# Cached keys turned in 32x32 blocks by VectorE, and sample scores computed as 4x4 tiles

## The reference, cut to what matters

```
s_past = (ql . cp^T + qp . kp^T) * ATTN_SCALE     # 32 x 4096, contraction over 256 + 64
s_new  = (ql . cn^T + qp . kn^T) * ATTN_SCALE     # 32 x 4, causal
p = softmax(concatenate([s_past, s_new]))
out = p_past . cp + p_new . cn                    # 32 x 256
```

## Time and profile before

| | |
|---|---|
| runs, median of 3 (lowest to highest) | 1405.34 us (1402.3 to 1409.27) |
| profiled execution | 1393.17 us |
| its span, first to last instruction | 1391.2 us |
| granted TensorE clock, mean | 0.990 of full speed |
| TensorE busy | 1354.7 us, 97% |
| VectorE, ScalarE, GpSimd busy | 810.8, 601.3, 725.7 us |

### The profile page before, as it was taken

How to read it: one execution, slowest core, us unless ns; L and a number is a source line. 1 busy time by engine, 2 the same in 40 slices (tenths; PEclk the granted TensorE clock), 3 DMA queues, 4 the chain that set the end, 5 groups by cost and what they waited for, 6 DMA issues and landing times.

```text
span 1391.2 us, 26303 instructions
## 1 busy us (share of the span) xinstructions
PE 1354.7 (97%) x11048; PEld 1261.1 (91%) x11048; DVE 810.8 (58%) x1232; ACT 601.3 (43%) x1021; POOL 725.7 (52%) x505
## 2 busy tenths in 40 slices
PE   7999889999999999999999999999999999999997
PEld 7877489999999999999899867678999999999997
DVE  6689557655545463766556656554685463645434
ACT  5121255443434443444666544342464444443432
POOL 3321153587878785333323444330437788887831
PEclk9999789999999999999999999999999999999999
DMA  5755302222233324332111477770223322222221
GB/s 215 209 149 147 109 31 92 92 92 91 92 100 100 104 92 147 128 92 66 35 35 53 182 296 261 269 260 7 92 75 101 98 92 92 92 91 92 91 91 65
DMA packets 108356, 160.66 MB, mean 115 GB/s; under 512 B 7696, under 2 KB 93968, under 8 KB 102992
## 3 DMA queue, kind: packets, MB, share of 16 engines
q1 hardware_dynamic: 100688, 116.50, 26.4%
q0 software_dynamic: 7168, 41.95, 8.0%
q10 hardware_dynamic: 384, 0.55, 0.1%
HBM read 146.22 MB, written 4.03 MB: 108 GB/s over the span
## 4 chain that ended last, share of the span: by engine, by line
PE 91%; DVE 4%; ACT 1%; issue 1%; DMA 1%; POOL 1%; ACTq 0%; POOLq 0%; SPq 0%; DVEq 0%
PE ps L1675 31%; PE ps L1805 21%; PE ps L1793 18%; PE ps L1935 5%; PE ps L1975 3%; PE ps L1713 2%; PE ps L2024 2%; PE ps L1726 1%; PE ps L2091 1%; ACT wh L717 1%; PE ps L2005 1%; POOL wl L589 1%; PE ps L2015 1%; PE ps L2033 0%; PE ps L1763 0%
## 5 line engine op out<-in xcount | busy, mean ns | idle before, releaser
L589 POOL TENSOR_TENSOR wl<-raw,wh 128x512 fp32r<-128x512 f32 (+2 forms) x252 | 438.0, 1740 | 441.8 <-ACT wh L717 441.6
L717 ACT ACTIVATE wh<-raw 128x512 fp32r<-128x512 f32 (+2 forms) x253 | 192.6, 762 | 386.3 <-PE ps L1675 184.5
L1675 PE MATMUL ps<-xh,wh 128*128 128x272 f32 x704 | 148.4, 292 | 12.6 <-DVE xl L1084 10.0
L589 POOL TENSOR_TENSOR wl<-wuv,wh 128x512 fp32r<-128x512 f32 x104 | 135.0, 1310 | 48.2 <-ACT wh L717 48.1
L1805 PE MATMUL ps<-mh,wh 128*128 128x272 f32 x768 | 158.7, 288 | 0.0
L1805 PE MATMUL ps<-mh,wl 128*128 128x272 f32 x768 | 158.6, 288 | 0.0
L1805 PE MATMUL ps<-ml,wh 128*128 128x272 f32 x768 | 158.3, 288 | 0.0
L1675 PE MATMUL ps<-xh,wl 128*128 128x272 f32 x704 | 145.6, 289 | 0.0
L1675 PE MATMUL ps<-xl,wh 128*128 128x272 f32 x704 | 145.4, 288 | 0.0
L1675 PEld LDWEIGHTS ps<-xh,wh 128*128 128x128 f32 x704 | 110.6, 190 | 17.7 <-POOL wl L589 9.9
L1805 PEld LDWEIGHTS ps<-ml,wh 128*128 128x128 f32 x768 | 120.4, 188 | 0.0
(11 more groups left out here) (315 smaller groups left out, 3029.3 us busy)
## 6 DMA issues: line engine op xcount, KB each, us to landing
raw<-w_up SPq DMA_DIRECT2D x32, 1024.0 KB, 5.4
raw<-w_down SPq DMA_DIRECT2D x32, 1024.0 KB, 5.1
raw<-w_pw SPq DMA_DIRECT2D x11, 1024.0 KB, 5.8
shifted<-ext SPq DMA_DIRECT2D x112, 66.5 KB, 2.0
raw<-w_o SPq DMA_DIRECT2D x4, 1024.0 KB, 5.7
raw<-w_dq SPq DMA_DIRECT2D x3, 1024.0 KB, 5.4
raw<-w_uq SPq DMA_DIRECT2D x4, 768.0 KB, 4.7
diag<-diags SPq DMA_DIRECT2D x7, 384.0 KB, 3.5
```

Source lines behind the costliest of these rows:

```text
L589: pf.tensor_tensor(weight(wl, u), weight_raw(u), f32(weight(wh, u)), ALU.subtract).then_inc(w_lo, 1)
L717: af.activation(weight(wh, u), weight_raw(u), ACT.Copy).then_inc(w_hi, 1)
L1675: m = tf.matmul(ps[:, bank_of(u) + bank, 0:width], w[:, k, :], a[:, k, part], start=(k == 0 and n == 0), stop=(k == nk - 1 and n == 2))
```

## The change

VectorE's 32x32 block transpose takes the place of TensorE's transposes. `turn_keys(n)` turns a chunk from SBUF to SBUF in two instructions (2048 and 512 elements in each partition) into one of three slots (`KT`); afterwards the 32 features of block l lie on the 32 partitions of a row group, for the positions that came from that group. The score of a set is then ten blocks of 32 features in four row groups: 32x32 tiles, each row group into its own PSUM bank (4 to 7), each set on its own 32 columns. The queries must stand on all four row groups: `queries_turned` makes them by 40 matmuls with the identity ahead of the rounds, and ScalarE copies them to `qrep`. TensorE's loop becomes scores, fold, probability transposes and values of the same round. The scores have one set of banks, so those of round i + 1 wait for the exp of round i. ScalarE takes over `collect`, `folds` and `values_out` from VectorE. There are six chunk buffers for seven, and the gathers from chunk 3 on stand behind the last head's outputs and ahead of two `low(u)`.

```diff
-CB = 7
-ORDER = (0, 2, 1, 3, 4, 5, 7, 6, 8, 9)
+CB = 6
+KT = 3
+QB = (KL + ROPE) // 32
+FOLDS = SETS * SPB + 1
...
+        SCORES = ps[:, 4:8, 0:P]
+        FOLDED = ps[:, 0, 0:KC * NS]
+        PROBS, VALUES = ps[:, 1, :], ps[:, 3, :]
...  GpSimd
             gather(2)
-            gather(3)
...
+            pool.wait_ge(pv_mm, NH)
+            for j in range(3, CB):
+                gather(j)
             low(U_WO)
             low(U_WO + 1)
-            pool.wait_ge(pv_mm, NH)
-            for j in range(4, NCH):
-                gather(j)
+            for i in range(NSC):
+                for j in (CB + 2 * i, CB + 2 * i + 1):
+                    if j < NCH:
+                        gather(j)
...  ScalarE
+            def queries_out(m):
+                act.wait_ge(q_mm, m + 1)
+                af.activation(qrep[:, 2 * m:2 * m + 2, :, :].rearrange("p l b q -> p (l b q)"), ps[:, QBANK[m], :], ACT.Copy).then_inc(q_out, 1)
...
+            def folds(b):
+                act.wait_ge(e_wn, b + 1)
+                if b > 1:
+                    act.wait_ge(e_mm, b - 1)
+                for s in range(SETS):
+                    for k in range(SPB):
+                        af.activation(fold_w[NS * s:NS * (s + 1), b % 2, k, :], ident32, ACT.Copy, scale=wn[:, s, k:k + 1]).then_inc(e_fold, 1)
...
             for i in range(NSC):
+                if i > 0:
+                    values_out(i - 1)
+                if i > 0 and i % SPB == 0:
+                    weights_out(i // SPB - 1)
                 act.wait_ge(ks_max, i + 1)
-                af.activation(ss[:, :], ps[:, 3 + i % 2, :], ACT.Exp, ...
+                af.activation(ss[:, :].rearrange("p (q g k) -> p g q k", q=SETS, g=GROUPS), SCORES.rearrange("p g (q k) -> p g q k", q=SETS), ACT.Exp, ...
...
-                keys(i + 1, (0, 2, 4, 6, 8))
                 probs_out(i)
-                if i % SPB == SPB - 1:
-                    weights_out(i // SPB)
+                if i % SPB == SPB - 1:
+                    collect(i // SPB)
+                elif i > 0:
+                    folds(i // SPB - 1)
+            weights_out(NB - 1)
+            folds(NB - 1)
+            values_out(NSC - 1)
...  VectorE
+            def turn_keys(n, parts=(0, 1)):
+                if n >= NCH:
+                    return
+                for k in parts:
+                    if k == 0:
+                        dve.wait_ge(c_in[n % CB], 32 * (n // CB + 1))
+                        if n >= KT:
+                            dve.wait_ge(ks_mm, (n - KT) // 2 + 1)
+                    df.transpose(keys_turned(n)[k], (latents(n), rotaries(n))[k]).then_inc(kt_out, 1)
...
             for i in range(NSC):
+                turn_keys(2 * i + 2)
+                if i > 0 and i % SPB == 0:
+                    weights_first(i // SPB - 1)
                 dve.wait_ge(ks_mm, i + 1)
-                link(df.tensor_reduce(m, ps[:, 3 + i % 2, :], AX.X, ALU.max))
+                link(df.tensor_reduce(m, SCORES, AX.XY, ALU.max))
                 df.tensor_scalar(nmx[:, i % SETS:i % SETS + 1], m, -SCALE, None, ALU.mult).then_inc(ks_max, 1)
-                keys(i + 1, (1, 3, 5, 7, 9))
+                if i > 0 and i % SPB == 0:
+                    weights_second(i // SPB - 1)
+                turn_keys(2 * i + 3)
...  TensorE
+            def queries_turned(m):
+                if m == QB // 2 - 1:
+                    pe.wait_ge(q_out, 1)
+                for e in range(2):
+                    l = 2 * m + e
+                    for g in range(GROUPS):
+                        o = tf.matmul(ps[32 * g:32 * g + 32, QBANK[m], e * NB * NS:(e + 1) * NB * NS], ident[:, 32 * (l % 4):32 * (l % 4) + 32],
+                                      qs[:, l // 4, :, :].rearrange("p b q -> p (b q)"), start=True, stop=True)
+                o.then_inc(q_mm, 1)
...
-            def scores_s(i, c):
+            def scores_s(i):
                 b = i // SPB
-                pe.wait_ge(kt_act, 5 * i + (4, 5, 5)[c])
-                pe.wait_ge(kt_dve, 5 * i + (3, 4, 5)[c])
-                for s in range(SETS):
-                    q = qs[:, c if c < KC else KC + s % 2, b, :]
-                    k = kt[:, 5 * (s // 2) + (2 * (s % 2) + c if c < KC else 4), :]
-                    m = tf.matmul(ps[NS * s:NS * (s + 1), 3 + i % 2, :], q, k, start=(c == 0), stop=(c == 2))
+                pe.wait_ge(kt_out, 4 * i + 4)
+                if i == 0:
+                    pe.wait_ge(q_out, QB // 2)
+                    pe.wait_ge(n_max, 2)
+                else:
+                    pe.wait_ge(ks_exp, i)
+                for l in range(QB):
+                    for s in range(SETS):
+                        for g in range(GROUPS):
+                            rows_ = slice(32 * g, 32 * g + 32)
+                            m = tf.matmul(ps[NS * s:NS * (s + 1), 4 + g, 0:P], qrep[rows_, l, b, :], keys_block(2 * i + s // 2, s % 2, l)[rows_],
+                                          start=(l == 0), stop=(l == QB - 1))
+                m.then_inc(ks_mm, 1)
...
             for i in range(NSC):
-                for c in range(3):
-                    scores_s(i, c)
-                if i > 0:
-                    values(i - 1)
+                scores_s(i)
...
                 if i > SPB and i % SPB == 1:
                     folded(i // SPB - 1)
-                keys(i + 1, range(9))
+                if i == NSC - 1:
+                    out_first(U_WO, range(3))
                 probs_turned(i)
-                keys(i + 1, (9,))
+                if i == NSC - 1:
+                    out_first(U_WO, range(3, 5))
+                values(i)
```

More of the change, by code:

```diff
@@ L909, in rotary_samples @@
             def rotary_samples(n):
-                if n == 0:
-                    act.wait_ge(zeros, 2)
                 act.wait_ge(rq_out, n + 1)
                 for e in range(2):
[L914 to L918, removed]
+                    af.activation(qs[0:64, KC, :, NT * (2 * n + e):NT * (2 * n + e + 1)],
+                                  t0[64 * e:64 * e + 64, NP:T].rearrange("p (b t) -> p b t", t=NT), ACT.Copy).then_inc(kcopy, 1)
             def project(h):
@@ L991, in _ @@
                 else:
-                    keys(0, (0, 2))
+                    for m in range(QB // 2):
+                        queries_out(m)
                 pv_()
@@ L1007, in probs_out, with values_out, collect @@
                 act.wait_ge(kp_mm, i + 1)
-                af.activation(pts[:, :, :].rearrange("p a b -> p (a b)"), ps[:, 5, :], ACT.Copy).then_inc(kp_out, 1)
+                af.activation(pts[:, :, :].rearrange("p a b -> p (a b)"), PROBS, ACT.Copy).then_inc(kp_out, 1)
+            def values_out(i):
+                act.wait_ge(ko_mm, i + 2)
+                if i >= SETS:
+                    act.wait_ge(e_mm, (i - SETS) // SPB + 1)
+                af.activation(oc[:, i % SETS, :], VALUES[:, 0:KL], ACT.Copy).then_inc(ko_out, 1)
+            def collect(b):
+                act.wait_ge(ks_exp, SPB * (b + 1))
+                act.wait_ge(n_exp, 2)
+                act.wait_ge(zeros, 4)
+                if b > 0:
+                    act.wait_ge(e_wn, b)
+                at, g = SPB * (b % 2), NS * (b % SETS)
+                for s in range(SETS):
+                    af.activation(e_g[:, s, :, :], st[NS * s:NS * (s + 1), at:at + SPB, :], ACT.Copy).then_inc(e_in, 1)
+                af.activation(e_g[:, SETS, 0, :], stn[g:g + NS, b // SETS, :], ACT.Copy).then_inc(e_in, 1)
+            def folds(b):
[5 more added lines that the diff above has]
+                        af.activation(fold_w[NS * s:NS * (s + 1), b % 2, k, :], ident32, ACT.Copy, scale=wn[:, s, k:k + 1]).then_inc(e_fold, 1)
+                g = b % SETS
+                af.activation(fold_new[NS * g:NS * (g + 1), g, :], ident32, ACT.Copy, scale=wn[:, SETS, 0:1]).then_inc(e_fold, 1)
             act.wait_ge(n_max, 2)
@@ L2023, in values @@
                         r = 2 * q + s % 2
[L2024 removed]
+                        m = tf.matmul(VALUES[NS * s:NS * (s + 1), 0:KL], pts[:, q, NS * s:NS * (s + 1)],
                                       latents(2 * i + s // 2)[:, r * KL:(r + 1) * KL], start=(q == 0), stop=(q == SETS - 1))
```

161 lines of the change are left out of this document (54 added, 107 removed).

## The result

The changed kernel took 1546.3 us (median of 4 runs, 1540.4 to 1553.6) against 1404.7 us (4 runs), a ratio of 1.102 [1.099, 1.105]: 142 us slower, where 1390 was forecast. Measured once more on another chip, the same kernel took 1507.8 us (1505.7 to 1513.8) against 1392.9, a ratio of 1.082 [1.079, 1.085].

A forecast was written before the change was run, and what follows sets the result against it. TensorE, 97% busy, was taken as the bound. 16 x 7.85 + 0.6 + 4.9 = 131.1 us against 161.0; prologue and clock losses left -15.7, from 1405.3 to about 1390. Range 1382 to 1401 (chance 0.42); 8 in 10, 1362 to 1440.

The forecast's parts named there:

- Scores as 32x32 tiles: TensorE's scores: 160 matmuls of 128 columns a round, each issued twice, forecast to take 2.9 us.
- S: Time of a round's score matmuls on TensorE, forecast at 2.9 us, near the low end of 2.2 to 9.0.
- Instructions must be fetched too: ... about 1.0 us each: TensorE's instruction queue: 256 instructions a fetch, 640 in the scores, 2.5 fetches or 2.6 us when they don't overlap.
- four loads ... start some 7 ns apart: TensorE's score loads: four stand in 0.13 us, so 320 loads a round would take 2.2 us.
- If all 16 tiles run side by side it is 20 sets, 2.2 us. ... If still only four run at once ... 9.0 us.: TensorE array in the scores: the low and high ends for a round, 2.2 us or 80 sets at 9.0 us.
- rival (c): Score tiles don't run together: eight at once 1405 to 1415 us, four 1477; chance 0.25, half for each.
- Nothing, but a floor.: Gathers beside the rounds: no cost, but 7.0 us of transfer a round, below which no round can come.
- "+3.4" and "+6.6": TensorE's clock: 3.4 us for a fall before round 0, 6.6 us for three more falls in the rounds.
- the 4.95 forecast: A round outside its scores: softmax gap, probability transposes, copy gap and values, 4.95 us together.
- rival (d): TensorE's clock at 1.2 GHz in the rounds: half of them low gives 1411 us, all 1443; chance 0.13.
- my 7.85: Length of a whole round in us: scores of 2.9 plus 4.95 for the rest.
- Order alone: Rounds ending with their own values: copy of probabilities 0.85 us less last key group 0.44 a round, 7 us in all.

The follow-up runs named there:

- a3: Changed kernel with its gathers, only five of the ten feature blocks multiplied in the scores: 1480.9 us, ratio 1.058.
- r1: The changed kernel run again, unaltered, on another chip: 1507.8 us, ratio 1.082.
- e2: Changed kernel with the gathers from chunk 6 on replaced by plain loads of the same sizes, issued by ScalarE: 1524.3 us, ratio 1.089.
- r2: Changed kernel without the gathers of chunks 6 to 31, run again on the chip of the unaltered rerun: 1469.4 us, ratio 1.054.
- b1: Kernel before, each score matmul of 512 columns cut into 16 of 32 columns: 1553.4 us, ratio 1.110.
- d1: Changed kernel with 80 score matmuls of 256 columns a round, for two of four sets, half the score tile left out: 1409.8 us, ratio 1.012.
- c1: Kernel before without the gathers from chunk 7 on, later rounds using old data: 1396.6 us, ratio 0.999.
- a2: Changed kernel without gathers of chunks 6 to 31, with filler matmuls in TensorE's gaps and the prologue: 1465.9 us, ratio 1.048.
- r3: Changed kernel with half of the feature blocks in the scores, run again on the chip of the unaltered rerun: 1398.2 us, ratio 1.004.
- o1: Kernel before with only the order changed, each round ending with its own values: 1417.3 us, ratio 1.013.
- h1: Changed kernel with sets cut otherwise, four neighbouring positions instead of every second one: 1512.3 us, ratio 1.085.
- h3: Changed kernel with 256 columns a score matmul, reading a set's keys twice: 1510.2 us, ratio 1.083.
- a1: Changed kernel without the gathers of chunks 6 to 31, later rounds computing on old data: 1471.4 us, ratio 1.052.
- e1: Changed kernel with one more wait on GpSimd, so gathers are issued after the next round's scores: 1499.2 us, ratio 1.070.

## Why the prediction was wrong, step by step

**The step that failed** is "Scores as 32x32 tiles", S = 2.9 us. It rests on three statements, each taken from rows.

*"Instructions must be fetched too: ... about 1.0 us each".* The 1.0 us is what a packet of the instruction queue occupies, not how often one can come. In the stage's fetch records of the kernels with small score matmuls, the two closest fetches start 3.2 to 3.6 us apart (4.4 in a3), though a packet takes 0.9 to 1.5. That is 13 ns an instruction; 640 are 8.4 us, and only those already fetched when the round begins come faster (up to 488 in a row in these traces). What holds the fetches apart was not tried. The term should have been some 6 to 9 us, not 2.6. S measured 9.0 in r1 and 6.9 without traffic.

*"four loads ... start some 7 ns apart".* Wrong as a pace too. The row shows four loads between waits of 0.30 us and says nothing of the matmuls that belong to them. The fastest long bursts of these tiles have a pair every 12.6 to 12.8 ns at full clock (232 pairs, e2 and r2), so 320 pairs are 4.1 us even when no instruction is waited for. That alone is above the 3.9 us from which the forecast had the change lose. 4.1 and the stalls, 41 / 16 = 2.6 us a round, make nearly all of the 6.9 us without traffic. What sets this pace wasn't tried; pairs of 32 columns on four tiles came every 8.3 ns (b1).

*"If all 16 tiles run side by side it is 20 sets, 2.2 us. ... If still only four run at once ... 9.0 us."* The tiles do run together (eight fully, d1), so rival (c) had the right place, and with four tiles the right S (9.0 and a round of 13.95; r1 has 9.0 and 16.7). That was luck: its mechanism was wrong. The Trainium skill (TensorE: Matmul & The Clock Gate, "Wait — 56ns, not 53.3ns?") gave 8 us from a floor of 25 ns between matmuls. By the measurement that floor isn't there on different tiles, since 232 score matmuls started 12.8 ns apart (e2); the size came out near for another reason. That section of the Trainium skill also names a path on which a matmul costs about 62 ns. The slow stretch, 0.757 / 12 = 63 ns an instruction, has that size; that it is that path no run here shows.

**Gathers: "Nothing, but a floor."** Wrong in this kernel. A fetch that falls among the gathers' packets starts late (a stop of 3.68 us with the DMA engines at 98.6%, for 1.3 to 1.8): 38 us in all (r1 against r2). 33 of them lie in the scores, some 20 as longer stalls; the mean clock was lower as well (0.76 for 0.83). On the first chip the slow stretch came on top, 142 us of loss for 115. In the kernel before the gathers cost nothing (c1).

**Clock: "+3.4" and "+6.6".** Undersized: the mean clock of the rounds was 0.76 in r1, 0.69 in the first profile, not a few falls. The rest of r1's round is 16.7 - 9.0 = 7.7 us for the 4.95 forecast, 43 us in 16 rounds, and values and transposes at 1.2 GHz are 3.64 - 1.73 + 1.13 - 0.44 = 2.6 us of those 2.7. A good part goes with the long scores: where scores are short (r3, d1) that rest is 6.0 to 6.5. Buying the clock back with filler saved 5.5 us, not clear of noise (a2). So rival (d) was a second cause and not the first: with the clock near full and without gathers, 69 us of the loss stayed (a2).

**Sum.** Of r1's round, 8.8 us over my 7.85, the scores are 6.1 and the rest 2.7; 16 x 8.8 = 141 us. Less the 10 that the forecast already had for the clock that makes 1390 + 131 = 1521, against 1508 measured beside a kernel before that was itself 12 us faster.

**What held.** VectorE's transposes: 2.31 us for 2048 elements (2.29 forecast) and 0.66 for 512 (0.69), never the bound in the rounds. The gaps: 1.77 us for the softmax (1.9), 0.67 for the copy (0.85); the forecast's terms for the rest of a round add up to 4.92, not 4.95, and nothing hangs on it. Rounds that end with their own values and short scores do come out near the forecast: r3, with S = 3.1, takes 9.5 us, and of the 1.7 over my 7.85 all but 0.2 lie outside the scores, where the mean clock was 0.85. First scores at 800.7 in one profile and 807.8 in the other (803.8 forecast). That transposes off TensorE were worth 4.5 us a round was never in doubt; their place was taken by 592 more instructions in the scores and by 2.5 us of gaps. *Order alone*: 7 us by my terms, 19 measured (o1).

## What to carry to other kernels

Count the instructions of a stretch as work of its own: here 256 TensorE instructions came no oftener than every 3.2 to 3.6 us, so a long stream needs on average 13 ns of array work or more behind each, and an fp32 matmul is four instructions. A price read from a few instructions in a pause is the price of a burst. Moving work to an idle engine is only half of a change; ask how many instructions the form needs that it forces on the busy one, and whether a wider matmul (fewer, longer) can do the same before anything else.

Compare times only with a kernel measured beside them on the same chip. Two of these experiments (h1, h3) were set up to explain 37 us that lay between two chips.

## What the runs showed of the hardware that I had not expected

- A fetch of TensorE's instructions shares the DMA engines with data: at 98.6 and 99.0% load a stall took 3.68 and 4.34 us for 1.3 to 1.8 without load. The packet is no longer in flight for it (0.9 to 1.3 us); it starts later, and TensorE goes on 1.2 to 1.6 us after it has landed.
- On some chips, TensorE got 12 instructions every 0.70 to 0.76 us while GpSimd issued indirect gathers, on 32x32 tiles and on four tiles of 128 rows alike (a1, b1, e1, first profile); on three others this never happened, with the same kernel on one of them (r1). Plain loads of the same size did not do it in an execution whose gathers did (e2).
- With 32x32 tiles in four row groups and two column groups, eight fp32 matmuls of 256 columns ran side by side (28.5 ns each).
- The kernel before, with scores cut small, shows the count alone: 48 score instructions a round 1397 us, 384 1453 us, 768 1553 us (1, 1.042 and 1.110 of the kernel before beside each).
